# One bias addition, norm statistics moved into the setup, the first tile's shift on VectorE, the first product behind the first turn

## The reference

```
mod = split(silu(c) @ ada_w[l] + ada_b[l], 6)        # and mod_c from c_ctx
h   = rms_norm(x) * norm1_g * (1 + mod[1]) + mod[0]  # context: mod_c
p   = h @ w_in[l]                                    # 1024 -> 3104 columns
y   = concat(gated linear attention, 8x16 window attention, differential attention)
x   = x + mod[2] * (y @ w_out[l])
h2  = rms_norm(x) * norm2_g * (1 + mod[4]) + mod[3]
x   = x + mod[5] * peer(h2)   # per token 8 heads x 16 rows of u and of v, fetched by index
```

## Time and profile before

| | |
|---|---|
| median of 3 runs | 4508.95 us (4507.74 to 4509.69) |
| the profiled execution | 4507.21 us, span 4505.4 us |
| busy in the span | PE 2254.4, DVE 2614.6, POOL 2604.7, ACT 462.0 us |
| DMA | 1496.76 MB, mean 332 GB/s |
| mean granted TensorE clock | 0.74 |

### The profile page before, as it was taken

One profiled execution on the slowest core, in us unless ns is written; L12 is line 12 of the kernel. 1 busy time (PEld: TensorE's weight loads), 2 busy tenths in 40 slices (PEclk: granted clock), 3 DMA queues, 4 the chain that ended last, 5 costly groups with the idle time before them and its releaser, 6 DMA issues. The chain is left out here.

```text
span 4505.4 us, 35616 instructions
## 1 busy us (share of the span) xinstructions
PE 2254.4 (50%) x11749; PEld 1085.6 (24%) x11749; DVE 2614.6 (58%) x5877; ACT 462.0 (10%) x944; POOL 2604.7 (58%) x2779
## 2 busy tenths in 40 slices
PE   7997887562052051151155787698454025035035
PEld 2434654220010010010013644475221001001001
DVE  2115568597945946846846700556867972963930
ACT  1004540110000000000000000352110000000000
POOL 1103305777777777777767563220777767767765
PEclk9997899886576576576577898789786568568556
DMA  6941026999999999999999998203999999999998
GB/s 221 277 163 38 22 111 222 400 409 409 410 407 409 409 399 409 409 399 409 409 402 407 400 399 337 103 2 114 370 409 409 410 409 409 410 405 400 410 409 332
DMA packets 454373, 1496.76 MB, mean 332 GB/s; under 512 B 60931, under 2 KB 94295, under 8 KB 448047
## 3 DMA queue, kind: packets, MB, share of 16 engines
q0 software_dynamic: 368640, 1342.34, 75.3%
q1 hardware_dynamic: 48104, 82.26, 5.3%
q10 hardware_dynamic: 37446, 69.88, 4.6%
HBM read 1476.58 MB, written 17.73 MB: 332 GB/s over the span
## 5 line engine op out<-in xcount | busy, mean ns | idle before, releaser
L2416 DVE CUSTOM_DVE_ANT_0 experts_V<-experts_V,experts_acc 128x1024 f32<-128x1024 f32 x512 | 621.1, 1220 | 488.2 <-DMA experts_V<-in_peer_u_dram,experts_expert 470.1
L1807 POOL DMA_INDIRECT experts_lent<-in_peer_u_dram,experts_expert x576 | 560.3, 973 | 581.6 <-DVE experts_expert L1556 385.8
L1814 POOL DMA_INDIRECT experts_V<-in_peer_v_dram,experts_turned x576 | 545.4, 947 | 262.1 <-issue 153.0
L2211 PE MATMUL experts_pair<-small,experts_w 128*128 128x128 f32 x12 | 5.6, 463 | 1278.6 <-DVE experts_w L2372 1177.9
L2416 DVE CUSTOM_DVE_ANT_0 experts_lent<-experts_lent,experts_acc 128x1024 f32<-128x1024 f32 x512 | 620.1, 1220 | 42.2 <-DMA experts_lent<-in_peer_u_dram,experts_expert 23.3
L2228 PE MATMUL experts_acc<-experts_lent,experts_U 128*32 128x512 f32 x1968 | 456.4, 816 | 330.2 <-DMA experts_lent<-in_peer_v_dram,experts_turned 174.8
L1807 POOL DMA_INDIRECT experts_V<-in_peer_u_dram,experts_expert x512 | 485.3, 948 | 172.3 <-issue 98.4
L1814 POOL DMA_INDIRECT experts_lent<-in_peer_v_dram,experts_turned x492 | 468.5, 952 | 185.5 <-issue 125.5
L2228 PE MATMUL experts_acc<-experts_V,experts_U 128*32 128x512 f32 x2304 | 386.6, 802 | 282.6 <-DMA experts_V<-in_peer_v_dram,experts_turned 282.6
L2211 PEld LDWEIGHTS experts_pair<-small,experts_w 128*128 128x128 f32 x12 | 2.1, 178 | 1282.0 <-DVE experts_w L2372 1179.7
L429 PE MATMUL proj_acc<-W,HT 128*128 128x512 f32 (+3 forms) x752 | 295.4, 547 | 5.5 <-DMA W<-in_w_in_dram 3.2
(11 more groups left out here) (299 smaller groups left out, 3794.3 us busy)
## 6 DMA issues: line engine op xcount, KB each, us to landing
proj_ada<-in_ada_w_dram ACTq DMA_DIRECT2D x40, 1024.0 KB, 5.7
W<-in_w_in_dram SPq DMA_DIRECT2D x9, 2048.0 KB, 14.8
experts_QT<-in_w_in_dram ACTq DMA_DIRECT2D x12, 960.0 KB, 18.4
experts_lent<-in_peer_u_dram,experts_expert POOLq DMA_INDIRECT x576
experts_V<-in_peer_v_dram,experts_turned POOLq DMA_INDIRECT x576, 12.9
PR<-in_ada_w_dram SPq DMA_DIRECT2D x8, 1024.0 KB, 17.3
experts_U<-in_w_out_dram SPq DMA_DIRECT2D x4, 2048.0 KB, 9.0
experts_V<-in_peer_wq_dram SPq DMA_DIRECT2D x4, 2048.0 KB, 18.0
```

The lines of the kernel that those rows point to most:

```text
L1807: pool.indirect_dma_start(into, None, u_rows, bass.IndirectOffsetOnAxis(ap=s.expert[:, j % 2, slot:slot + 1], axis=0)).then_inc(done, 16)
L1814: pool.indirect_dma_start(into, None, v_rows, bass.IndirectOffsetOnAxis(ap=s.turned[:, q % 2, at:at + 1], axis=0)).then_inc(done, 16)
L2211: nc.tensor.transpose(tr[:, P:2 * P], s.w[:], m.ident).then_inc(wtr, 1)
L2416: nc.vector.tensor_tensor_reduce(out=rows, in0=rows, in1=s.H[:, tiles[0]] if q == 0 and k < FROM_BANK else h_bank(), scale=1.0, scalar=0.0 ...
```

## The change

In the setup, VectorE first clears the whole 128x512 tile of bias rows and the whole PSUM bank of the strips. ScalarE's bias loads wait for the first clearing, TensorE's first strip for the second. One addition over 128 partitions then takes the place of the four over two rows each. VectorE takes the mean of squares between the two scales, ScalarE takes the root (with its table load) between the two shift copies, and VectorE takes the reciprocal last, all into a new tile `first_stat` that lives as long as the program and is allocated before most others. With `ready`, `norm_modulate` uses it and computes no statistics. In every call of `norm_modulate` VectorE adds the shift of the first tile itself, and GpSimd begins with the second. In layer 0 the first product stands directly behind the first turn; the second and third keep their places.

```diff
@@ setup, ScalarE
+                act.wait_ge(blank, 1)
                 ada_bias(act, m, rows, 0, 0, biases)
...
                     nc.scalar.activation(sh[:, stream]..., spread[:, 0:2], ACT.Copy).then_inc(shifts, 1)
-                act.wait_ge(squared, NT)
+                    if stream == 0:
+                        act.wait_ge(mean, 1)
+                        nc.scalar.activation(m.first_stat[:, 1], m.first_stat[:, 0], ACT.Sqrt).then_inc(root, 1)
@@ setup, TensorE
                 pe.wait_ge(silu_col, 1)
+                pe.wait_ge(cleared, 1)
...
-                        pe.wait_ge(added, strip + 1)
+                        pe.wait_ge(added, 1)
@@ setup, VectorE
+                nc.vector.memset(rows[:], 0.0).then_inc(blank, 1)
                 nc.vector.memset(m.pad[:], 0.0).then_inc(padded, 1)
+                nc.vector.memset(acc[:], 0.0).then_inc(cleared, 1)
...
-                for strip in range(4):
-                    row = rows[32 * strip:32 * strip + 2]
-                    nc.vector.tensor_tensor(row, row, acc[32 * strip:32 * strip + 2], ALU.add).then_inc(added, 1)
+                nc.vector.tensor_tensor(rows[:], rows[:], acc[:], ALU.add).then_inc(added, 1)
...
+                    if stream == 0:
+                        dve.wait_ge(squared, NT)
+                        nc.vector.tensor_scalar(m.first_stat[:, 0], m.ssq[:], 1.0 / D, EPS, ALU.mult, ALU.add).then_inc(mean, 1)
+                dve.wait_ge(root, 1)
+                nc.vector.reciprocal(m.first_stat[:, 2], m.first_stat[:, 1])
@@ norm_modulate, VectorE
+        factor = m.first_stat[:, 2] if ready else stat[:, 3]
...
+            if i == 0:
+                dve.wait_ge(hs, 1)
+                if not ready:
+                    dve.wait_ge(shifts, 16 * len(streams))
+                nc.vector.tensor_tensor(row, row, sh[:, 0 if t < CT else 1], ALU.add).then_inc(hb, 1)
@@ norm_modulate, GpSimd
         for i, t in enumerate(tiles):
+            if i == 0:
+                continue
             pool.wait_ge(hs, i + 1)
@@ project
             def early(pe, i):
-                if 0 < i <= EARLY:
+                if i == 0 and EARLY:
+                    product(pe, 0)
+                elif 1 < i <= EARLY:
                     product(pe, i - 1)
@@ build
+        m.first_stat = sb("firststat", [P, 3, NT])
```

More of the change, by code:

```diff
@@ L205, in setup @@
         padded, silu_tr, silu_col = (st.sem(x) for x in ("padded", "silutr", "silucol"))
+        blank, cleared, mean, root = (st.sem(x) for x in ("blank", "cleared", "mean", "root"))
         x_in, ctx_in = st.sem("xin"), st.sem("ctxin")
@@ L325, in _ @@
             nc.scalar.activation(junk, m.X[:, t], ACT.Square, accum_out=m.ssq[:, t:t + 1]).then_inc(ssq, 1)
-        act.wait_ge(mean, 1)
-        nc.scalar.activation(stat[:, 2, t0:t1], stat[:, 1, t0:t1], ACT.Sqrt).then_inc(root, 1)
+        if not ready:
+            act.wait_ge(mean, 1)
+            nc.scalar.activation(stat[:, 2, t0:t1], stat[:, 1, t0:t1], ACT.Sqrt).then_inc(root, 1)
         for i, t in enumerate(tiles):
@@ L343, in _ @@
             dve.wait_ge(ssq, n)
[L344 to L348, removed]
+            nc.vector.tensor_scalar(stat[:, 1, t0:t1], m.ssq[:, t0:t1], 1.0 / D, EPS, ALU.mult, ALU.add).then_inc(mean, 1)
+            dve.wait_ge(root, 1)
+            nc.vector.reciprocal(stat[:, 3, t0:t1], stat[:, 2, t0:t1]).then_inc(inv, 1)
+            dve.wait_ge(inv, 1)
             dve.wait_ge(coef, len(streams))
@@ L359, in _ @@
                 dve.wait_ge(trs, i - 1)
-            nc.vector.scalar_tensor_tensor(out=h[:, i % 2 if own else t], in0=m.X[:, t], scalar=stat[:, 3, t:t + 1],
+            row = h[:, i % 2 if own else t]
+            nc.vector.scalar_tensor_tensor(out=row, in0=m.X[:, t], scalar=factor[:, t:t + 1],
                                            in1=sc[:, 0 if t < CT else 1], op0=ALU.mult, op1=ALU.mult).then_inc(hs, 1)
+            if i == 0:
+                dve.wait_ge(hs, 1)
+                if not ready:
+                    dve.wait_ge(shifts, 16 * len(streams))
+                nc.vector.tensor_tensor(row, row, sh[:, 0 if t < CT else 1], ALU.add).then_inc(hb, 1)
             if i:
```

## The result

The changed kernel takes 4426.83 us, the median of four runs (4423.52 to 4430.54). The kernel before took 4508.34 us beside it (4507.29 to 4509.69). The ratio is 0.9818, with an interval of 0.9805 to 0.983: 81.5 us faster, where 2.6 were predicted, and far outside the range. The profiled run took 4424.43 us, span 4422.6. One execution of the first kernel of Experiment 1, 4500.46 us, fell into a slower state of the chip and is left out of its median.

The account below looks back on a forecast made before the run. Gathers fill the DMA engines for 75.3% of the span, untouched by the edits; the front gains 3.45 us at the first turn less 0.85, so 2.6: 4508.95 becomes 4506.3 us, range 4502.5 to 4511.5.

Parts of the forecast that it names:

- Moved tiles: Later buffers, gathers' included, move; if a row's cost changes, 1%, 34 us either way; chance 0.05 faster, 0.03 slower.
- Clearing first: Setup: ScalarE's bias loads wait for VectorE's clearing, so its loads and square sums come 0.6 us later (0.3 to 0.8).
- The queue did not catch up: Setup: if the queue of ScalarE's loads caught up, the square sums' delay would be 0 and the sum 0.6 us better.
- One bias addition: Setup: one addition of 0.7 us gains 2.1 us on VectorE, of which nothing is left because ScalarE is late next.
- Statistics in the setup: Setup ends 0.35 us later; the projection's first scaling starts at 45.82 instead of 47.18, 1.35 earlier.
- First shift on VectorE: First projection: VectorE adds the first tile's shift in 1.22 us; TensorE turns it at 48.45, 3.45 before 51.91.
- Product behind the turn: First projection: first product starts at 51.25 instead of 55.99, takes 9.2 us instead of 8.16; second starts at 62.25.
- The product stays slow: Rival: TensorE's first product runs wholly at the lower clock, 14.1 us instead of 9.2, giving 4511.2; chance 0.05.
- Second layer: One tile's shift is 1.1 us faster, but products wait for weights: gain 0; rival gaining 1.1 more, 4505.2, chance 0.09.
- The gain is taken back: Rival: a modulation weight transfer later in the first projection is set by the clock, ending the gain, 4508.95; chance 0.07.

Follow-up runs that it names:

- Experiment 1: Two kernels against the one before: an unused 96-byte tile alone, 4426.65 us, ratio 0.982; the edits with every tile at its old address, 4510.5 us, ratio 1.0001.

## Why the prediction was wrong

**The step that failed** is the first one: "None of the edits touches their number, size or order. So the change can act in the program's first 80 us and at one tile of the second layer". Number, size and order are not all that a transfer's cost hangs on; its address does as well, and that the change moved. A tile that nothing uses, with every instruction as before, took 4426.65 us, and the edits at the old addresses 4510.5. "Moved tiles" saw the mechanism, down to the multiple of 256 bytes, and gave it 0.05 for faster because "nothing in the rows shows such a dependence". No row could: in the kernel before every row lies off, so its trace has no other case to compare. That was no evidence against, only an absence. Its price of 1% was too small as well: the two stages lost 74 of 3384 us, 2.2%.

**Clearing first** was right: loads issued at 1.44 (1.38 forecast), a clearing of 0.48 (0.49), square sums that end at 39.96 (39.8). The queue did not catch up.

**One bias addition** was right: the spread products run together from 34.86 for 2.09 us, the second stream starts at 40.97 (40.87), and ScalarE is what is late.

**Statistics in the setup** were right: table load and root lie between the copies, and the first scaling starts at 45.91 (45.82).

**First shift on VectorE** was right: 1.23 us (1.22), first turn at 48.51 (48.45).

**Product behind the turn** had the right start, 51.31 (51.25). Its length was 8.66 in the profiled run instead of 9.2, which is the 0.5 us between the 3.1 and the 2.6 of this pair of traces. In the other four traces with the new order it was 9.09 to 9.27, so 9.2 was well taken. The 8.16 that it was compared with was not: it is the longest of the eight traces with the old order, whose mean is 7.5. The move costs the product about 1.5 us and not 1.0, and the front's gain is nearer to 1.7 than to 2.6 or 3.1 (Experiment 1). That the pair of traces agrees so well with the sum is in part luck. "The product stays slow" didn't happen in any. Two of the recorded sums are slightly off: the first turn adds up to 48.48, and the upper end of the range to 4511.9.

**Second layer** was forecast at 0, and the runs can't tell it from 0. With the edits alone the tile is turned earlier (2801.11 instead of 2802.14), TensorE then waits longer for weights, 4.75 us instead of 3.17, and the stage behind starts at 2844.34, where it started at 2843.63:

```profile
2826.02 16.44 PE L448 MATMUL proj_acc<-W,HT 128*128 128x512 f32 x32 [4.75 <-DMA W<-in_w_in_dram]
```

That fits the forecast, but the wait scatters as much without the edits: 1.33 us in the kernel with rows 128 bytes off, 4.00 in the one with 192, 1.00 in the one with the tile alone. In the changed kernel it is 2.39, and that stage starts 2.45 us sooner after the first square of its tile than before. The kernel with rows 128 bytes off is 2.8 us sooner by the same measure, so the 2.45 can't be put down to the edits or to the addresses.

**The gain is taken back** isn't seen: the next stage starts 4.0 us earlier (368.36 against 372.36), 2.5 with the edits alone. Without the edits it starts between 369.34 and 374.97 in the eight traces, and at 370.50 in the changed kernel traced again, so these rows fit a gain that is handed on but don't measure it.

## What to carry to other kernels

Ask of every change that adds, drops or resizes a buffer which later buffers it moves, and where the targets of the largest transfers then begin; a tile that nothing uses tells this apart from the edit in one run. Put the targets of gathers and loads of large rows at multiples of 256 bytes. Size a gain of a few microseconds from several traces of either kernel and not from one pair. When a dependence can't show in a trace because the trace has one case only, give it a chance for what it would move, and not for its absence from the rows.

## What was not expected of the hardware

Rows of 4 KB that land off a multiple of 256 bytes arrive at 409 to 410 GB/s instead of 420 to 422, in gathers (at every offset tried, from 4 to 224) and in loads on SyncE's queue (at 32, 64 and 128). By the slope below the ceiling, such a row costs about 5% more transfer time, an estimate. The ceiling of some 420 GB/s is why moving half of the rows in the gathers by themselves saved as much as moving all; GpSimd's issuing, one gather of 128 rows each 1.242 us or 422 GB/s, lies so close to it that the two weren't separated. And the first product after a pause took 7.03 to 8.16 us behind two turns (eight traces) and 8.66 to 9.27 behind one (five), against 7.03 to 7.11 for the next in all of them.
